# Paged keys as tiles of four pages, by indirect DMA, with 32x32 transposes on VectorE

## What is computed

```python
# per sequence b of 8, 8 new tokens, 8 heads of 128, past = 16 pages of 128 rows
k_past = cache_k[page_table]          # (8, 2048, 8, 128), 4 KB a row
logits = einsum('bthd,bshd->bths', q, k_all) * HEAD_DIM ** -0.5
logits = where(selected, logits + bias, -inf)      # top 256 keys of each token
out = einsum('bths,bshd->bthd', softmax(logits), v_all)
```

## Time and profile before

| | us |
|---|---|
| three runs | 1593.25, 1597.6, 1598.45 |
| median | 1597.6 |
| the profiled execution: its time, its span | 1593.25, 1593.2 |
| first key page transposed (L1197) | 464.6 |
| first round: logits done, first and last value page | 580.2, 595.8, 705.8 |
| second round: logits done, first and last value page | 812.3, 828.4, 929.0 |

### The profile page before, as it was taken

The page is one execution under the profiler, slowest core; times in us unless marked ns, Lnnn a source line. Parts: engine busy times, 40 slices in busy tenths (PEclk is TensorE's granted clock), DMA queues, the critical chain, the costliest instruction groups (busy, mean ns, idle before and its releaser), DMA issues.

```text
span 1593.2 us, 32571 instructions
## 1 busy us (share of the span) xinstructions
PE 1471.7 (92%) x13518; PEld 1334.5 (84%) x13518; DVE 762.0 (48%) x1030; ACT 511.5 (32%) x818; POOL 234.5 (15%) x371
## 2 busy tenths in 40 slices
PE   7999998979979989899998998899799999999995
PEld 4867798957867778797777998799699999999995
DVE  5288699496514540025540135543555555552123
ACT  4243223324323341023341122122344455442121
POOL 3423234154210000000000000321000110000000
PEclk8899999989999999999999999899799999999998
DMA  5415223122159979999869976133322233223221
GB/s 173 149 27 159 65 80 113 57 96 73 49 188 369 332 249 342 383 358 329 310 223 402 363 258 240 34 125 104 113 80 80 80 90 95 83 98 102 79 83 60
DMA packets 179278, 266.58 MB, mean 167 GB/s; under 512 B 20522, under 2 KB 136539, under 8 KB 178043
## 3 DMA queue, kind: packets, MB, share of 16 engines
q1 hardware_dynamic: 167947, 243.95, 44.5%
q0 software_dynamic: 5104, 11.11, 2.1%
q10 hardware_dynamic: 6080, 9.44, 1.6%
HBM read 240.28 MB, written 24.18 MB: 166 GB/s over the span
## 4 chain that ended last, share of the span: by engine, by line
PE 77%; DVE 8%; DMA 5%; ACT 3%; SPq 2%; issue 2%; POOL 2%; ACTq 0%; DVEq 0%
PE PS L987 14%; PE PS L989 13%; PE PS L988 13%; PE PS L1197 8%; PE PS L1210 4%; PE PS L1245 3%; PE PS L1319 3%; PE PS L1318 3%; PE PS L1317 3%; DMA R<-in_cache_v 3%; PE PS L1028 2%; PE PS L1029 2%; PE PS L1030 2%; PE PS L1173 1%; PE PS L1120 1%
## 5 line engine op out<-in xcount | busy, mean ns | idle before, releaser
L987 PE MATMUL PS<-xn_hi,WH 128*128 128x288 f32 (+1 forms) x1424 | 430.7, 302 | 16.0 <-DVE xn_lo L1614 13.2
L988 PE MATMUL PS<-xn_lo,WH 128*128 128x288 f32 (+1 forms) x1424 | 424.7, 298 | 0.0
L989 PE MATMUL PS<-xn_hi,WL 128*128 128x288 f32 (+1 forms) x1424 | 424.6, 298 | 0.0
L987 PEld LDWEIGHTS PS<-xn_hi,WH 128*128 128x128 f32 (+1 forms) x1424 | 271.1, 190 | 33.1 <-issue 22.2
L988 PEld LDWEIGHTS PS<-xn_lo,WH 128*128 128x128 f32 (+1 forms) x1424 | 271.9, 191 | 0.0
L989 PEld LDWEIGHTS PS<-xn_hi,WL 128*128 128x128 f32 (+1 forms) x1424 | 271.6, 191 | 0.0
L582 DVE TENSOR_TENSOR WL<-W,WH 128x2048 fp32r<-128x2048 f32 (+2 forms) x69 | 145.7, 2112 | 241.6 <-ACT WH L1358 241.6
L1358 ACT ACTIVATE WH<-W 128x2048 fp32r<-128x2048 f32 (+2 forms) x81 | 145.1, 1791 | 90.2 <-PE PS L1319 74.9
L1197 PE MATMUL PS<-CST,R 128*128 128x128 f32 x1024 | 142.7, 283 | 9.8 <-DMA R<-in_cache_k 9.5
L1793 DVE COPY RB<-PS 128x512 f32<-128x512 f32 x128 | 88.3, 691 | 115.7 <-PE PS L1197 115.7
L1197 PEld LDWEIGHTS PS<-CST,R 128*128 128x128 f32 x1024 | 112.1, 143 | 35.9 <-issue 25.7
(11 more groups left out here) (257 smaller groups left out, 2423.2 us busy)
## 6 DMA issues: line engine op xcount, KB each, us to landing
R<-in_cache_k SPq DMA_DIRECT2D x128, 512.0 KB, 5.3
R<-in_cache_v SPq DMA_DIRECT2D x128, 512.0 KB, 7.0
W<-in_w_in SPq DMA_DIRECT2D x30, 1024.0 KB, 5.4
W<-in_w_up SPq DMA_DIRECT2D x44, 512.0 KB, 4.6
W<-in_w_down SPq DMA_DIRECT2D x16, 704.0 KB, 4.4
x_scratch<-xT SPq DMA_DIRECT2D x2, 2304.0 KB, 9.0
W<-in_w_branch_a SPq DMA_DIRECT2D x4, 1024.0 KB, 7.9
W<-in_w_branch_b SPq DMA_DIRECT2D x4, 1024.0 KB, 6.1
```

The costliest lines, as they stand in the source:

```text
L987: pe.matmul(out, hi[:, k, cols], x.hi_block(n)[:, tokens], start=first, stop=False)
L988: pe.matmul(out, hi[:, k, cols], x.lo_block(n)[:, tokens], start=False, stop=False)
L989: return pe.matmul(out, lo[:, k, cols], x.hi_block(n)[:, tokens], start=False, stop=last)
```

## The change

The keys come as 16 tiles `KR` of 2 MB a round, four pages each, in two buffers over the same eight slots. GpSimd issues four indirect DMAs for a tile (`load_keys`); DMA r brings to partition 32 bb + i the row 32 r + i of the page of sequence bb. The row numbers (`KROW`) are computed once from the page table on GpSimd. VectorE transposes a half tile (four heads, 2048 elements a partition) by one instruction, in blocks of 32x32, into one of three buffers `KTB`: partition 32 bb + d, with the keys in natural order along the free side. TensorE multiplies it with block-diagonal queries `QB`, one product for each head and each quarter j of the head's 128 dimensions; the contraction runs over the four sequences and 32 dimensions, and the four quarters add up. Tiles `kl` and `o` move from pairs to single banks. ScalarE makes the queries and takes over the mask's way through DRAM. Side tiles: two at the start, five in each key stage, two in each softmax, four in the first value stage, three in the second, one at the end. SP keeps the value pages and the weights.

```diff
+    SIDE_K = [2, 5, 8, 11, 14]
+    SIDE_V = [{8: 1}, {8: 1}, {8: 1}, {8: 1}, {8: 1}, {8: 1}, {8: 1}, {}]
...
-    put_side(('start',), 3)
+    put_side(('start',), 2)
...
+        for kp in SIDE_K:
+            put_side(('K', G, kp), 1)
+        put_side(('softmax', G, 0), 2)
...
-        QZ = R3[:, 4352:6400].rearrange("p (h b c) -> p h b c", h=H, b=8)
+        QB = R3[:, 4352:6400].rearrange("p (g h j c) -> p g h j c", g=2, h=H, j=4)
         kTn = blocks(R3[:, 6400:7424], H)
-        KTb = [blocks(RB[:, 1024 * i:1024 * i + 1024], H) for i in range(2)]
+        KR = [blocks(R1[:, 4096 * i:4096 * i + 4096], 4) for i in range(2)]
+        KTB = [blocks(a, 4) for a in (RB[:, 0:2048], R3[:, 0:2048], R3[:, 2048:4096])]
...
-            G, kind, n = (seq - 8) // 128, (seq - 8) // 64 % 2, (seq - 8) % 64
-            if kind == 0:
-                e.wait_ge(single_filled, single.slots['kp', G, n, 1][0] + 1)
+            G, kind, n = seq // 128, seq // 64 % 2, seq % 64
+            if kind == 0 and n >= 8:
+                e.wait_ge(S_("k_transposed"), 32 * G + 2 * (n // 4 - 1))
+            elif kind == 0:
+                e.wait_ge(S_("v_pages_used"), 64 * G - 4 + 4 * (n // 4))
+            elif n < 8:
+                e.wait_ge(S_("k_transposed"), 32 * G + 30 + 2 * (n // 4))
             else:
-                e.wait_ge(S_("v_pages_used"), 64 * G + n + 1)
+                e.wait_ge(S_("v_pages_used"), 64 * G + n - 7)
...
+        def load_keys(e, G, kp):
+
+            page_freed(e, 128 * G + 4 * kp)
+            for r in range(4):
+                e.indirect_dma_start(out=KR[kp % 2][:, r, :], out_offset=None,
+                                     in_=cache_k[0].rearrange("n p h d -> (n p) (h d)"),
+                                     in_offset=bass.IndirectOffsetOnAxis(ap=KROW[:, 16 * G + kp:16 * G + kp + 1],
+                                                                         axis=0), element_offset=32 * D * r)\
+                    .then_inc(key_in[kp % 2], 16)
...
+            for bb in range(4):
+                sp.dma_start(PROW[32 * bb:32 * bb + 32, :].rearrange("p (g k) -> p g k", g=2),
+                             bass.AP(page_table.tensor, NPAGES * bb, [[0, 32], [4 * NPAGES, 2], [1, NPAGES]]))\
+                    .then_inc(S_("rows_in"), 16)
...
             side_loads('start')
-            for seq in range(4):
-                load_page(seq)
-
-            sp.wait_ge(S_("sample_mask"), 1)
-            sp.dma_start(mask_scr, S).then_inc(S_("mask_out"), 16)
-            sp.wait_ge(S_("mask_out"), 16)
-            for j in range(4):
-                sp.dma_start(MG[32 * j:32 * j + 32, :], mask_scr[0:32, :]).then_inc(S_("mask_in0"), 16)
-            for seq in range(4, 8):
-                load_page(seq)
+
             for G in range(2):
-                for n in range(64):
-                    load_page(128 * G + n + 8)
+                for kp in range(NPAGES):
+                    side_loads('K', G, kp)
+                for n in range(8):
+                    load_page(sp, 128 * G + 64 + n)
                 side_loads('softmax', G, 0)
                 side_loads('softmax', G, 1)
                 for b in range(4):
                     for kp in range(NPG):
                         if kp < NPAGES:
-                            load_page(128 * G + 64 + 16 * b + kp + 8)
+                            if 16 * b + kp + 8 < 64:
+                                load_page(sp, 128 * G + 64 + 16 * b + kp + 8)
...
+            pool.wait_ge(S_("rows_in"), 64)
+            pool.wait_ge(S_("consts_in"), 16)
+            link(pool.tensor_copy(RB[:, 32:64], PROW[:, :]))
+            link(pool.tensor_scalar(RB[:, 32:64], RB[:, 32:64], 128.0, const('lane')[:, 0:1], ALU.mult, ALU.add))
+            link(pool.tensor_copy(KROW[:, :], RB[:, 32:64]))
...
+            pool.memset(QB, 0.0).then_inc(S_("queries_cleared"), 1)
+            load_keys(pool, 0, 0)
             link(pool.memset(kTn[:, :, TS:P], 0.0))
             link(pool.tensor_copy(kTn[:, :, 0:TS], kT[:, :, TP:T]))
             link(pool.tensor_copy(QN, qT[:, :, TP:T]))
             pool.memset(ST[0:1, 110:111], 0.0).then_inc(S_("ring_free"), 1)
-            link(pool.memset(QZ, 0.0))
-            for b in range(NB_):
-                c = b % 4
-                last = pool.tensor_copy(QZ[:, :, b, 8 * c:8 * c + 8], qT[:, :, TP + 8 * b:TP + 8 * b + 8])
-            last.then_inc(S_("sample_queries"), 1)
+            load_keys(pool, 0, 1)
...
+            for kp in range(2, NPAGES):
+                load_keys(pool, 0, kp)
             drained(pool, 'kl', 0, NPG - 1)
             for j in range(4):
                 pool.dma_start(MG[32 * j:32 * j + 32, :], mask_scr[32:64, :]).then_inc(S_("mask_in1"), 16)
+            for kp in range(NPAGES):
+                load_keys(pool, 1, kp)
...
+                for kp in range(NPAGES):
+                    if (G, kp) == (0, 0):
                         pe.wait_ge(S_("sample_queries"), 1)
...
+                    claim(pe, 'kl', G, kp)
+                    for u in range(2):
+                        pe.wait_ge(S_("k_transposed"), 32 * G + 2 * kp + u + 1)
+                        keys = KTB[(2 * kp + u) % 3]
+                        for j in range(4):
+                            for c in range(4):
+                                last = pe.matmul(bank('kl', G, kp)[32 * c:32 * c + 32, P * u:P * u + P],
+                                                 QB[:, G, 4 * u + c, j, :],
+                                                 keys[:, :, P * c + 32 * j:P * c + 32 * j + 32],
+                                                 start=(j == 0), stop=(j == 3))
+                        if u == 0:
+                            last.then_inc(S_("k_half_used"), 1)
+                        else:
                             done(last, 'kl', G, kp)
+                    sides('K', G, kp)
...
+            act.wait_ge(S_("queries_cleared"), 1)
+            for G in range(2):
+                for bb in range(4):
+                    for j in range(4):
+                        t = TP + 32 * G + 8 * bb
+                        last = act.activation(QB[32 * bb:32 * bb + 32, G, :, j, 8 * bb:8 * bb + 8],
+                                              qT[32 * j:32 * j + 32, :, t:t + 8], ACT.Copy)
+            last.then_inc(S_("sample_queries"), 1)
+            act.wait_ge(S_("sample_mask"), 1)
+            act.dma_start(mask_scr, S).then_inc(S_("mask_out"), 16)
             sides('start')
+            act.wait_ge(S_("mask_out"), 16)
+            for j in range(4):
+                act.dma_start(MG[32 * j:32 * j + 32, :], mask_scr[0:32, :]).then_inc(S_("mask_in0"), 16)
             for G in range(2):
-                for n in range(64):
-                    filled(act, 'kp', G, n, 0)
-                    act.activation(KTb[n % 2][:, 0:4, :], blocks(bank('kp', G, n, 0), 4), ACT.Copy)\
-                        .then_inc(drains('kp', G, n, 0), 1)
+                for kp in range(NPAGES):
+                    sides('K', G, kp)
...
+                def transposed(kp):
+
+                    dve.wait_ge(key_in[kp % 2], 64 * (8 * G + kp // 2 + 1))
+                    for u in range(2):
+                        n = 2 * kp + u
+                        if n in (1, 2):
+                            if G == 0:
+                                filled(dve, 'pv', H - 1)
+                            else:
+                                filled(dve, 'o', 0, 3)
+                        if n >= 3:
+                            if n % 2 == 0:
+                                filled(dve, 'kl', G, (n - 3) // 2)
+                            else:
+                                dve.wait_ge(S_("k_half_used"), 16 * G + (n - 3) // 2 + 1)
+                        elif G and n == 0:
+                            filled(dve, 'kl', 0, NPAGES - 1)
+                        dve.transpose(KTB[n % 3], KR[kp % 2][:, :, 512 * u:512 * u + 512])\
+                            .then_inc(S_("k_transposed"), 1)
+
+                for kp in range(NPAGES):
+                    transposed(kp)
+                    if kp >= 2:
+                        logits(kp - 2)
+                    if kp == 13:
                         drained(dve, 'kl', G, 11)
                         dve.tensor_reduce(EARLY, LS[:, :, 0:12 * P], AX_X, ALU.max)
+                    splits('K', G, kp)
+                logits(14)
```

91 lines of the change are left out of this document (31 added, 60 removed).

## The result

The changed kernel takes 1619.87 us (median, 1618.03 to 1623.1) against 1595.42 us of the kernel before in the same comparison: ratio 1.0154, interval 1.013 to 1.0178. It is slower by 1.5%. The forecast was 1547 us, 73 us less. The profiled execution's span is 1618.8 us.

A forecast was written before the change was run, and what follows sets the result against it. Key stages were taken as bound by TensorE, value stages as TensorE waiting for pages. Stage by stage, the last value page moved from 929.0 to 880.9 us: 1593.2 - 48 = 1545 us, forecast 1547 as median, range 1508 to 1605.

The forecast's parts named there:

- Transposes, 2.2 us each: Key stages, VectorE: each transpose of 2048 elements a partition takes 2.2 us, 4.4 us for a tile of four pages.
- Rival 4: Key stages: VectorE's transposes run at half rate, 4.4 us each, 10.1 us a tile, + 115 us, 1662 us; chance 0.05.
- GpSimd, 1.3 us an issue: Key stages: each indirect DMA costs GpSimd 1.3 us to issue, 5.2 us for a tile of four.
- rival 3: Key stages: GpSimd's issues bind; at 2.4 us each a tile takes 9.6 us, + 99 us, 1646 us; chance 0.08.
- Rival 5: Key stages: GpSimd can't write descriptors while VectorE transposes, so a tile costs 9.6 us, 1646 us; chance 0.04.
- The period, 6.5 us: Key stages: issues, landing, transposes and hand-over form a loop shared by two buffers, 6.5 us for a key tile.
- The start: Start of the first key stage: the first key tile landed at 455.3 us, the second at 462.3, the third at 469.6.
- Side tiles free in the key stage: Key stages: they carry ten side tiles within the 6.5 us period, which leaves the value stages bound by DMA.
- Values, 83 us each: Value stages: bound by DMA, 32.7 MB at 415 GB/s are 78.7 us, plus 3.5 and 0.8 us; second one 82.5.
- Softmax, 24.0 and 24.5 us: Softmax stages: one more side tile each, 6.3 us plus 2.1 for the lower clock, on today's 15.6 and 16.1 us.
- Second key stage, 106 us: Second round's keys: first tile issued at 661.5 us, landed 670, 15 periods to 767.5, end 773.9.
- Rival 2: Key stages: side tiles at the lower clock, 12.8 us, make TensorE the bound; + 45 us, 1592 us; chance 0.15 (shared with slower issues).

The follow-up runs named there:

- quarters_back: quarters with the side tiles where they stood before the change, none in the key stages and nine in each value stage: 1559.11 us.
- quarters: Changed kernel with four 1 MB key buffers, mask sent first, half tiles transposed by two 1024-element instructions, products still 128 columns wide: 1572.71 us.
- mask_first: Changed kernel with ScalarE sending the mask out before its query copies and reading it back before the start's side-tile drains: 1613.89 us.
- sides_back: Changed kernel with the side tiles where they were before the change: 1612.55 us, ratio 1.0143 to the kernel before.
- sliced: Changed kernel with side tiles of key and value stages cut into pieces, put behind half tiles and pages: 1598.60 us.
- quarters_sliced: Changed kernel with the edits of quarters and of sliced together: 1547.38 us, ratio 0.9718 to the kernel before.
- half_mask_back: Changed kernel with four 1 MB key buffers, 64-column products, mask sent first, and side tiles where they stood before the change: 1627.08 us.

## Why the prediction was wrong, point by point

- *What bounds the kernel now: right.* TensorE in the key stages; without its 131 us of transposes a key stage of 75 us exists (quarters_back), against 99.
- *Transposes, 2.2 us each: right*, 2.29 us, between ends of 1.15 and 4.4. Rival 4 falls. 1.1 ns an element is the rate of the earlier trace rows. The Trainium skill, "Vector Engine (DVE) Microarchitecture Reference", section "3.8 The reshape front-end and per-opcode configuration", says that the transposing array keeps up one element a cycle for each lane; the row fits that, with 2289 ns for 2048 elements.
- *GpSimd, 1.3 us an issue: right*, 0.94 and 0.30 between two. Single issues took 1.91 to 2.53 us; rival 3 falls.
- *Rival 5, GpSimd locked out: not seen.* In quarters VectorE transposes for most of the stage and the issues beside it take 0.94 us. The long ones lie beside L593, the subtraction with two inputs: one of 1.98 us began at 489.08 us in L593's 487.96 to 490.24. The Trainium skill, "SBUF — State Buffer", section "Who interferes with whom", has both halves: an instruction with at most one SBUF input outside the two-port modes leaves GpSimd alone, one with two SBUF inputs contends with GpSimd's reads. The trace agrees with the first half: in quarters no issue beside a transpose alone took over 1.02 us. With the second it agrees in part: in the changed kernel all five long issues began within a subtraction and ended some 0.8 us behind it, but the issue before each of them, which ran beside the same subtraction in part, took 0.94 us. I had used the section for the half that didn't apply.
- *The period, 6.5 us: the step that failed.* The form was right (issues, landing, transposes, over two buffers), and so were the issues (3.9 us, measured 3.7 to 4.8). The landing was too small: I took 3.8 to 5.3 us from the earlier trace rows. The first of these rows is a store from SBUF in a quiet queue and no load at all, the second a key page in a stream that waited for TensorE. Here it is 6.9 us in the mean, with three other key DMAs, the other buffer's, weights and stores under way. The turn is 15.9 us and not 13.0. A tile takes 7.93 us in the first key stage (13 tiles) and 7.73 in the second (15 tiles), against 6.5: 37 us of the 73. I had written that the forecast is wrong from 8 us a tile on, by rival 3, 4 or 5; it was wrong just below that, and by none of them.
- *"6.5 us is hardly less than today's": the judgement that failed with it.* A ring at 0.85 of DMA share was read as nearly the DMA limit. Every microsecond in it counts half, and it has no slack for what it meets: side tile, split, mask.
- *The start: wrong by 13 us.* Third tile at 483.05 instead of 469.6 us. Two terms had been put at nothing. ScalarE's query copies held up a weight's rounding, and with it VectorE's subtraction and the first transposes: 459.83 instead of 455.3 us. And the mask's bytes on ScalarE's queue met the third tile's in the DMA engines: a landing of 14.61 us, 10.01 in mask_first.
- *Side tiles free in the key stage: wrong.* sides_back against the changed kernel: no difference; quarters_back against quarters: they cost 14 us. The value stages gave 3 us for four side tiles fewer between the value pages (103.4 to 100.1), and 10 us for six fewer (100.6 to 91.0).
- *Values, 83 us each: 100 and 92 us.* Two causes: bursts behind a whole side tile, which sliced takes away, and a throughput that I had at 415 GB/s from 2 us of the earlier trace rows; over a whole stage of quarters_sliced at a share of 0.99 it is 385 GB/s, over 80 us of sliced 397. At 385 it is 6 us of the 83.
- *Softmax, 24.0 and 24.5 us: 19.5 and 18.1.* Two side tiles there ran at clock 1.00, no 2.1 us for a cold start, and the second tile filled gaps of the softmax itself. The miss is on the good side, 11 us.
- *Second key stage, 106 us: 131 us* from the last value product on. 15 periods of 7.7 us are 18 us of the excess. Its first tile began at 718.18 us, 5 us after the last value product, where 2.5 us had been forecast.
- *Rival 2, the clock: in part.* A side tile that began at the lower level took 8.1 us, as summed (8.4), not 12.8. 1592 us was nearer to the outcome by luck: its mechanism (TensorE full in the key stage) is not what happened: TensorE waited 33.2 us for VectorE there.

The sum of the misses from the changed kernel's profile: first key stage and start +33.2, softmax -4.5 and -6.4, values +17.1 and +10.0, second key stage +24.2: 73.6 us. The profile lies 73.8 us over the forecast for it (1618.8 against 1545), the median 73 over 1547.

## What to carry to other kernels

When transfers, an engine and the issuing of the next transfer form a ring over few buffers, sum the turn with landing times under load, and take no credit for an engine or a DMA share below 1: more and smaller buffers over the same memory (here four of 1 MB for two of 2 MB) were worth as much as halving the transposes. Cut the tile where the loads and releases are, and leave the products as wide as they were. Work put in as a filler should come in pieces between the waits, not whole, and only where its engine has time to spare.

## What the runs showed of the hardware that was not expected

- Two queues of direct DMAs into 32 partitions each: 240 GB/s with the DMA engines busy throughout, against 361 GB/s at 0.98 in quarters for indirect DMAs over 128 partitions with the same 4 KB rows.
- The landing of a 512 KB indirect DMA, the fourth of its tile, takes 5.4 to 9.2 us in the first key stage; it was 14.6 us beside the mask's traffic and 10.0 without it.
- In the changed kernel five issues of an indirect DMA on GpSimd took 1.91 to 2.53 us instead of 0.94; all five began while VectorE ran its subtraction with two inputs (L593). Beside a transpose they take 0.94 us.
- TensorE can stall in a sequence of small products with nothing that the trace names as the releaser: 30.7 us in 80 with 64 moving columns (half_mask_back), 19 us in 505 with 128 (the changed kernel), none in quarters and quarters_back.
- Over 80 to 90 us at a share of 0.99 to 1.03 the DMA engines moved 378 to 397 GB/s (quarters_sliced, sliced); 423 was seen only over 2 us.
